# Seven-product multiplication in the up projection of a first MLP, with plain pairs in front that make its factors

## The reference

```python
h2 = rms_norm(x, ffn_norm)
u = causal_dwconv(h2 @ w_up, conv_w, conv_b)      # w_up: 1024 x 5632, three taps along the tokens
a, bval = jnp.split(u, 2, axis=-1)
return x + (jax.nn.silu(a) * bval) @ w_down       # w_down: 2816 x 1024
```

## Time and profile before

| | |
|---|---|
| Time, median of 3 runs (lowest to highest) | 1718.55 us (1718.5 to 1719.16) |
| The profiled execution: own time, span | 1718.6 us, 1716.8 us |
| TensorE matmul busy | 1704.7 us (99%), 9425 matmuls |
| TensorE weight loads | 1440.6 us (84%) |
| VectorE, ScalarE, GpSimd busy | 62%, 51%, 56% |
| Granted TensorE clock, mean | 0.999 |
| Mean transfer rate | 98 GB/s |

### The profile page before, as it was taken

How to read it: one execution, slowest core, us unless ns; L and a number is a source line. 1 busy time by engine, 2 the same in 40 slices (tenths; PEclk the granted TensorE clock), 3 DMA queues, 4 the chain that set the end, 5 groups by cost and what they waited for, 6 DMA issues and landing times.

```text
span 1716.8 us, 27243 instructions
## 1 busy us (share of the span) xinstructions
PE 1704.7 (99%) x9425; PEld 1440.6 (84%) x9425; DVE 1061.0 (62%) x2084; ACT 868.3 (51%) x1498; POOL 963.1 (56%) x1095
## 2 busy tenths in 40 slices
PE   9999999999999999999999999999999999999998
PEld 7778888888888778888989898977777889898988
DVE  6875755555311455568757575867776676757576
ACT  5665555555322444435545444546655554545355
POOL 5543655555555434357666666755554665656666
PEclk9999999999999999999999999999999999999999
DMA  5221333332334322223323323233322242333332
GB/s 192 74 68 61 100 98 98 97 93 93 108 95 137 104 68 83 74 74 123 99 98 99 105 96 106 64 128 116 105 97 70 87 133 91 109 99 98 99 98 74
DMA packets 48662, 167.91 MB, mean 98 GB/s; under 512 B 5376, under 2 KB 6672, under 8 KB 48528
## 3 DMA queue, kind: packets, MB, share of 16 engines
q1 hardware_dynamic: 48272, 166.05, 30.2%
q10 hardware_dynamic: 288, 0.52, 0.1%
HBM read 164.31 MB, written 2.24 MB: 97 GB/s over the span
## 4 chain that ended last, share of the span: by engine, by line
PE 90%; DVE 6%; ACT 2%; issue 1%; DMA 0%; POOL 0%; SPq 0%; DVEq 0%; ACTq 0%
PE bank L736 18%; PE bank L1444 6%; PE bank L1453 6%; PE bank L1445 6%; PE bank L661 5%; PE bank L660 5%; PE bank L666 5%; PE bank L1033 5%; PE bank L1034 5%; PE bank L1038 5%; PE bank L754 3%; PE bank L760 3%; PE bank L755 3%; PE bank L1086 2%; PE bank L1081 2%; PE bank L1080 2%
## 5 line engine op out<-in xcount | busy, mean ns | idle before, releaser
L507 POOL TENSOR_TENSOR w_lo<-stage,w_hi 128x256 fp32r<-128x256 f32 x872 | 672.2, 803 | 571.7 <-ACT w_hi L1506 317.5
L1506 ACT ACTIVATE w_hi<-stage 128x1024 fp32r<-128x1024 f32 x218 | 229.4, 1052 | 200.9 <-PE bank L1081 54.7
L660 PE MATMUL bank<-xn_hi,w_hi 128*128 128x512 f32 x544 | 211.8, 389 | 0.0
L661 PE MATMUL bank<-xn_lo,w_hi 128*128 128x512 f32 x544 | 211.7, 389 | 0.0
L736 PE MATMUL bank<-xn_hi,w_hi 128*128 128x512 f32 x464 | 189.1, 407 | 0.0
L736 PE MATMUL bank<-xn_lo,w_hi 128*128 128x512 f32 x464 | 181.8, 392 | 0.0
L2890 DVE TENSOR_TENSOR x<-x,bank 128x256 f32<-128x256 f32 (+1 forms) x217 | 97.4, 455 | 89.3 <-PE bank L1453 86.6
L1453 PE MATMUL bank<-arena 128*128 128x256 f32 x896 | 146.6, 283 | 0.0
L1033 PE MATMUL bank<-xn_hi,w_hi 128*128 128x512 f32 x352 | 137.1, 389 | 0.0
L1034 PE MATMUL bank<-xn_lo,w_hi 128*128 128x512 f32 x352 | 136.9, 389 | 0.0
L666 PE MATMUL bank<-xn_hi,w_lo 128*128 128x512 f32 x544 | 135.0, 389 | 0.0
(11 more groups left out here) (374 smaller groups left out, 3719.3 us busy)
## 6 DMA issues: line engine op xcount, KB each, us to landing
stage<-weights SPq DMA_DIRECT2D x219, 512.0 KB, 3.6
prob<-pairs SPq DMA_DIRECT2D x32, 512.0 KB, 3.6
stage<-pairs SPq DMA_DIRECT2D x32, 512.0 KB, 3.6
bias<-table SPq DMA_DIRECT2D x11, 896.0 KB, 6.4
out<-y SPq DMA_DIRECT2D x8, 256.0 KB, 2.2
x<-x_in SPq DMA_DIRECT2D x3, 512.0 KB, 7.6
bias<-swa_table SPq DMA_DIRECT2D x4, 256.0 KB, 4.4
con<-consts SPq DMA_DIRECT2D x1, 640.0 KB, 9.8
```

The lines of the kernel that those rows point to most:

```text
L507: ins = nc.gpsimd.tensor_tensor(w_lo[:, p_, ks], stage[:, p_, ks], w_hi[:, p_, ks].bitcast(F32), ALU.subtract)
L660: pe.matmul(G[p_][:], w_hi[:, p_, k], hi[:, k], start=(first and k == ks[0]), stop=False)
L661: mm = pe.matmul(G[p_][:], w_hi[:, p_, k], lo[:, k], start=False, stop=False)
L1506: act.activation(w_hi[:, p_], stage[:, p_], ACT.Copy).then_inc(hi_ready, 1)
```

## The change

Five of the 22 up pairs stay as they were. The other 17 become "quads": a pair's weights, 1024 by 256, are taken as four blocks of 512 by 128, the activations as four blocks of 512 features by 256 tokens, and seven products of 4 x 3 matmuls of 256 columns take the place of 48 matmuls of 512.

- During plain pairs 0 to 3 the activations' factors are made, one block of features a pair: VectorE multiplies two blocks of `x` by the norm's weight and rstd (already scaled, so the quads need no scaling) and forms four differences (`factors_first`, `factors_second`); ScalarE copies them to high parts (`factor_highs`, 256 and 1536 columns); VectorE (256 and 512 columns) and GpSimd (1024 columns in one instruction) make the low parts in the next pair.
- In a quad VectorE forms four sums of weight blocks and two low parts, ScalarE seven high parts and a copy, GpSimd five low parts. TensorE makes the products in the order `UP_ORDER` in four regions of PSUM. ScalarE copies four of them out, VectorE adds four (`c_00`, `c_01`, `c_1`), and the convolution follows.
- GpSimd multiplies the halves (`f_made_of`) instead of VectorE. Results stay in float32 and are split only at the end (`f_high`, `f_low`), since the factors lie where the parts will go. The first down tile therefore runs its matmuls of high and low weights by high results first and all those by low results last.
- The `Fori` loops of this stage are written out.

The core of the diff (indentation reduced):

```diff
-N_UP1 = 2 * NF1
+N_PLAIN = 5
+FACTORS_AT = [0, 1, 2, 3]
+Q_UP = NF1 - N_PLAIN
+N_UP1 = 2 * N_PLAIN
...
+UP_ORDER = [HI_A11, HI_S1, HI_A12, HI_S2, HI_S4, HI_A22, HI_S3]
+SLOT_ORDER = [HI_A11, HI_S1, HI_A12, HI_S2, HI_S4, HI_S3, HI_A22]
...
+factor = arena[:, N_IN_ARENA:2 * NF1].rearrange("p (c a r) s -> p c a (r s)", c=7, a=2)
+factor_parts = [arena_raw[:, 6:10].rearrange("p k s -> p (k s)"), v_tok[:].rearrange("p a b t f -> p (a b t f)")]
...
+f_home = [arena[:, N_IN_ARENA + 4 * c + b] for c in F_FREE for b in range(4)]
+f1_hi = f_home[0:NF1]
...
+def factor_lows(k):
+
+    pool.wait_ge(ffh_ready, 2 * k + 2)
+    ks = slice(k * HS, (k + 1) * HS)
+    nc.gpsimd.tensor_tensor(factor[:, F_T1:, 1, ks], factor_parts[k % 2][:, 2 * S:].rearrange("p (c s) -> p c s", c=4),
+                            factor[:, F_T1:, 0, ks].bitcast(F32), ALU.subtract).then_inc(factor_low, 1)
...
+def f_made_of(i):
+
+    pool.wait_ge(silu_done, i + 1)
+    pool.wait_ge(conv_2, 2 * i + 2)
+    nc.gpsimd.tensor_tensor(f1[i], conv_acc(i, 0), conv_acc(i, 1), ALU.mult).then_inc(f_made, 1)
...
+for i in range(N_PLAIN - 1):
+    split_lo(T_MLP1 // 2 + i + 1, 0)
+    if i:
+        f_made_of(i - 1)
+    if i - 1 in FACTORS_AT:
+        factor_lows(FACTORS_AT.index(i - 1))
+    split_lo(T_MLP1 // 2 + i + 1, 1)
+f_made_of(N_PLAIN - 2)
+if N_PLAIN - 2 in FACTORS_AT:
+    factor_lows(FACTORS_AT.index(N_PLAIN - 2))
...
+for q in range(Q_UP):
+    up_low(HI_S3, q)
+    if q == 0:
+        up_low(HI_A22, 0)
+    if q + 1 < Q_UP:
+        up_low(HI_A11, q + 1)
+    else:
+        split_lo(T_DOWN1 // 2, 0)
+        split_lo(T_DOWN1 // 2, 1)
+    f_made_of(N_PLAIN + q - 1)
+    if q + 1 < Q_UP:
+        for k in (HI_A12, HI_S4, HI_A22):
+            up_low(k, q + 1)
...
+def up_product(q, k):
+
+    region = R2 if k in (HI_A12, HI_A22) else R5 if k in (HI_S1, HI_S4) else R1[q % 2][:, 0:HS]
+    fresh = k in (HI_A11, HI_S1, HI_A12, HI_A22)
...
+    pe.wait_ge(slot_high, UP_HIGH_AT[k, q])
+    if k == HI_A11:
+        if q == 0:
+            pe.wait_ge(ffh_ready, FFH_PREP)
+            pe.wait_ge(ff_ready, FF_PREP)
+            pe.wait_ge(tab_sb, 2)
+        if q < 2:
+            pe.wait_ge(conv_2, 2 * (N_PLAIN - 2) + q + 1)
+        else:
+            pe.wait_ge(up_moved, moved_at(q - 2, U3_COPY))
+    elif k == HI_S1:
+        if q == 0:
+            pe.wait_ge(factor_low, QUADS)
+        else:
+            pe.wait_ge(product_added, 4 * (q - 1) + C_01)
+    elif k == HI_A12 and q:
+        pe.wait_ge(product_added, 4 * (q - 1) + C_10)
+    elif k == HI_S2:
+        pe.wait_ge(up_moved, moved_at(q, P1_COPY))
+    elif k == HI_S4:
+        pe.wait_ge(up_moved, moved_at(q, P5_COPY))
+    elif k == HI_A22:
+        pe.wait_ge(product_added, 4 * q + C_00)
+    elif k == HI_S3:
+        pe.wait_ge(up_moved, moved_at(q, U2_COPY))
+    for i in range(QUADS):
+        w, cols = up_hi[k][:, i * P:(i + 1) * P], slice(i * HS, (i + 1) * HS)
+        pe.matmul(region, w, factor[:, f, 0, cols], start=(fresh and i == 0), stop=False, skip_group_check=True)
+        pe.matmul(region, w, factor[:, f, 1, cols], start=False, stop=False, skip_group_check=True)
+    if k in UP_SUM_LOW:
+        pe.wait_ge(sum_made, N_SUM * q + UP_SUM_LOW[k])
+    else:
+        pe.wait_ge(slot_low, UP_LOW_AT[k, q])
+    for i in range(QUADS):
+        w, cols = up_lo[k][:, i * P:(i + 1) * P], slice(i * HS, (i + 1) * HS)
+        mm = pe.matmul(region, w, factor[:, f, 0, cols], start=False, stop=(i == QUADS - 1), skip_group_check=True)
+    mm.then_inc(product_done, 1)
...
+for i in range(1, N_PLAIN):
+    for p_ in range(2):
+        up_tile(i, p_)
+for q in range(Q_UP):
+    for k in UP_ORDER:
+        up_product(q, k)
...
+    if d == 0:
+        for s_, ks in pieces:
+            for k, f in ks:
+                if f in POOL_LOWS:
+                    pe.wait_ge(factor_low, QUADS + POOL_LOWS.index(f) + 1)
+                else:
+                    pe.wait_ge(ff_ready, FF_PREP + DVE_LOWS.index(f) + 1)
+                mm = pe.matmul(G[0][:], down_hi(T_DOWN1 + s_)[:, k], f1_lo[f], start=False, stop=(f == NF1 - 1))
+            mm.then_inc(hi_free if ks[-1][0] == KD - 1 else down_done, 1)
...
+def factor_highs(k):
+
+    act.wait_ge(factor_made, k + 1)
+    ks = slice(k * HS, (k + 1) * HS)
+    act.activation(factor[:, F_B11, 0, ks], factor_parts[k % 2][:, 0:HS], ACT.Copy).then_inc(ffh_ready, 1)
+    act.activation(factor[:, F_B21:, 0, ks], factor_parts[k % 2][:, S:].rearrange("p (c s) -> p c s", c=6),
+                   ACT.Copy).then_inc(ffh_ready, 1)
...
+def p5_copied(q):
+    act.wait_ge(product_done, N_PROD * q + UP_AT[HI_S1])
+    act.wait_ge(conv_2, 2 * (N_PLAIN + q))
+    if q == Q_UP - 1:
+        act.wait_ge(sum_made, N_SUM * q + UP_SUM_LOW[HI_S1])
+    act.activation(up_bank(N_PLAIN + q, 1)[:, HS:S], R5, ACT.Copy).then_inc(up_moved, 1)
...
+split_hi(T_MLP1 // 2 + 1, 0)
+for i in range(N_PLAIN - 1):
+    conv_0_of(i, 0)
+    silu(i)
+    split_hi(T_MLP1 // 2 + i + 1, 1)
+    conv_0_of(i, 1)
+    if i < N_PLAIN - 2:
+        split_hi(T_MLP1 // 2 + i + 2, 0)
+    if i in FACTORS_AT:
+        factor_highs(FACTORS_AT.index(i))
+act.wait_ge(tables_saved, 80)
+up_copy(0)
+act.wait_ge(ff_ready, FF_PREP)
+act.wait_ge(factor_low, QUADS)
+up_high(HI_A11, 0)
+conv_0_of(N_PLAIN - 1, 0)
+for k in (HI_S1, HI_A12, HI_S2, HI_S4):
+    up_high(k, 0)
+up_copy(1)
+for q in range(Q_UP):
+    i, more = N_PLAIN + q, q + 1 < Q_UP
+    if q:
+        u3_copied(q - 1)
+    if not more:
+        split_hi(T_DOWN1 // 2, 1)
+    silu(i - 1)
+    if q == 0:
+        conv_0_of(i - 1, 1)
+    up_high(HI_S3, q)
+    p1_copied(q)
+    if q:
+        conv_0_of(i - 1, 1)
+    else:
+        up_high(HI_A22, 0)
+    if more:
+        up_high(HI_A11, q + 1)
+    else:
+        f_high(0)
+        f_high(1)
+    p5_copied(q)
+    if more:
+        up_high(HI_S1, q + 1)
+        up_high(HI_A12, q + 1)
+    else:
+        for f in range(2, 6):
+            f_high(f)
+    u2_copied(q)
+    if more:
+        up_high(HI_S2, q + 1)
+        up_high(HI_S4, q + 1)
+    else:
+        f_high(6)
+        f_high(7)
+        f_high(8)
+    conv_0_of(i, 0)
+    if more:
+        up_high(HI_A22, q + 1)
+    if q + 2 < Q_UP:
+        up_copy(q + 2)
...
+def factors_first(k):
+
+    e = factor_parts[k % 2]
+    if k >= 2:
+        dve.wait_ge(ffh_ready, 2 * (k - 1))
+        dve.wait_ge(ff_ready, 2 * (k - 1))
+        dve.wait_ge(factor_low, k - 1)
+    b11, b12, b21, b22, t1, t3, t2, t4 = parts(k)
+    dve.scalar_tensor_tensor(out=e[:, 0:S], in0=x[:, k], scalar=pcol("ffn_norm", k, k + 1), in1=rstd[:],
+                             op0=ALU.mult, op1=ALU.mult)
+    dlink(dve.scalar_tensor_tensor(out=e[:, S:2 * S], in0=x[:, k + 4], scalar=pcol("ffn_norm", k + 4, k + 5), in1=rstd[:],
+                                   op0=ALU.mult, op1=ALU.mult))
+    dve.tensor_tensor(t1, b12, b11, ALU.subtract)
+    dlink(dve.tensor_tensor(t3, b22, b12, ALU.subtract))
+
+def factors_second(k):
+
+    b11, b12, b21, b22, t1, t3, t2, t4 = parts(k)
+    dlink(dve.tensor_tensor(t2, b22, t1, ALU.subtract))
+    dve.tensor_tensor(t4, b21, t2, ALU.subtract).then_inc(factor_made, 1)
...
+def c_00(q):
+
+    dve.wait_ge(up_moved, moved_at(q, P1_COPY))
+    dve.wait_ge(product_done, N_PROD * q + UP_AT[HI_A12])
+    dve.wait_ge(conv_2, 2 * (N_PLAIN + q) - 1)
+    if q == Q_UP - 1:
+        dve.wait_ge(sum_made, N_SUM * Q_UP)
+    dve.tensor_tensor(up_bank(N_PLAIN + q, 0)[:, 0:HS], p1_copy, R2, ALU.add).then_inc(product_added, 1)
...
+for i in range(N_PLAIN - 1):
+    scaled(i, 0)
+    conv(i, 0)
+    if i - 1 in FACTORS_AT:
+        factor_lows(FACTORS_AT.index(i - 1))
+    if i in FACTORS_AT:
+        factors_first(FACTORS_AT.index(i))
+    scaled(i, 1)
+    conv(i, 1)
+    if i in FACTORS_AT:
+        factors_second(FACTORS_AT.index(i))
+scaled(N_PLAIN - 1, 0)
+if N_PLAIN - 2 in FACTORS_AT:
+    factor_lows(FACTORS_AT.index(N_PLAIN - 2))
+for k in (HI_S1, HI_S3, HI_S2, HI_S4):
+    up_sum(0, k)
+conv(N_PLAIN - 1, 0)
+up_sum_low(0, HI_S1)
+up_sum_low(0, HI_S2)
+for q in range(Q_UP):
+    i, more = N_PLAIN + q, q + 1 < Q_UP
+    if q:
+        c_1(q - 1)
+    else:
+        scaled(i - 1, 1)
+        conv(i - 1, 1)
+    if more:
+        up_sum(q + 1, HI_S1)
+        up_sum(q + 1, HI_S3)
+        up_sum(q + 1, HI_S2)
+    if q:
+        conv(i - 1, 1)
+    c_00(q)
+    if more:
+        up_sum(q + 1, HI_S4)
+        up_sum_low(q + 1, HI_S1)
+        up_sum_low(q + 1, HI_S2)
+    else:
+        for f in range(3):
+            f_low(f)
+    c_01(q)
+    if not more:
+        f_low(3)
+    conv(i, 0)
+f_low(4)
+c_1(Q_UP - 1)
+f_low(5)
+f_low(6)
+conv(NF1 - 1, 1)
+for f in DVE_LOWS[7:]:
+    f_low(f)
+dve.wait_ge(f_made, NF1)
```

406 lines of the change are left out of this document (296 added, 110 removed).

## The result

The changed kernel takes 1727.76 us (median of 5 runs, 1726.84 to 1728.53), the kernel before 1718.58 us beside it (1718.5 to 1719.16): a ratio of 1.0052, 95% interval 1.004 to 1.0063. It is slower by half a per cent, inside the range of 1710 to 1729 and on the side that had the largest chance, but 5 us above the forecast of 1722.7. The profiled execution took 1727.2 us, with a span of 1725.4 (before: 1716.8). So 8.6 us have to be found.

What follows compares the result with a forecast made beforehand. TensorE was taken to bound the kernel (90% of the chain of waits). Against 1718.6 us, -13.8 + 12.0 + 3.4 + 1.4 + 1.0 = +4.0 us, forecast 1722.7 us, range 1710 to 1729.

Steps and rivals of the forecast that it cites:

- TensorE's saving: Up stage: 17 pairs at 10.89 us become seven products at 10.08 us, saving 13.8 us if TensorE never waits.
- The plain pairs: Factor-making pairs: a VectorE-ScalarE loop of 14.1 us delays the first product from 253.5 to 265.5, costing 12.0 us.
- rival C: Plain pairs: VectorE stands for GpSimd's whole instruction once in each of three loops, 6.9 us more, 1729.6 us; chance 0.09.
- Rival A: Plain pairs: small disturbance, first product only 3 to 6 us late, total faster at 1712.8 us; chance 0.33.
- The first two quads: Start of the quads: TensorE waits 2.4 us, then about 1.3, for VectorE's additions and copy; 3.4 us, ends 1 and 5.
- The steady quads: Remaining 15 quads: an engine-order loop of 10.17 us against TensorE's 10.08, costing 1.4 us, ends 0 and 6.
- The first down tile: First down tile: VectorE's low parts end at 12 to 17 us, TensorE wants the last at 15; 1.0 us, ends 0 and 3.
- the sign of being wrong: First down tile: the forecast is wrong if it takes over 3 us more than 66 x 0.227.

Runs made afterwards that it cites:

- n7: Seven plain pairs instead of the changed kernel's five, factors still made in pairs 0 to 3; 1721.32 us.
- n7_last: Changed kernel with seven plain pairs, factors in 0, 1, 3, 4, later high parts, low parts on VectorE, down-tile reordering and early matmuls, earlier weight split; 1711.91 us.
- highs_later: Changed kernel with ScalarE making a factor block's high parts behind the next pair's first convolution term instead of ahead of it; 1729.64 us.
- awake: Changed kernel with thirty unused matmuls behind the last plain pair, keeping TensorE busy during its wait before the first product; 1727.82 us.
- pieces: Changed kernel with GpSimd's 1024-column low-part instruction for a factor block cut into four of 256 columns; 1727.93 us.
- end_order: Changed kernel with all results' low parts on VectorE, and VectorE's last quad addition and ScalarE's high part of result 11 moved earlier; 1726.36 us.
- n6: Six plain pairs instead of the changed kernel's five, factors still made in pairs 0 to 3; 1728.80 us.

## Why the prediction was right, and where it was not

**TensorE's saving** was right: one product starts each 1.44 us, and the steady quads have no gap.

**The plain pairs** were right in mechanism: a closed loop through VectorE and ScalarE, slowed by GpSimd, sets the first product. That the start came out so close (265.5 against 264.97) is partly luck, as three parts were off in both directions. The last differences of pair 0 were done at 215.2 and not at 218.2: the convolution ended 0.7 us earlier, nothing disturbed that pair, where 1.8 was put in, and its steps took 0.5 less. The three loops behind it took 44.3 us (16.2, 13.8 and 14.2, to 259.4) and not 42.3, as one of them paid rival C's price. The way from there to the first product took 5.5 and not 5.0. Inside a loop the two terms were off as well: the loop alone is 11.0 and not 11.7, the disturbance 2.8 and not 2.4. n7 and n7_last show that this delay was the cost ahead of the steady quads. Rival A ("the disturbance is small") is out; rival C's mechanism is real, and how often it strikes hangs on small shifts of timing: a small move of ScalarE's order (highs_later) made it happen three times.

**The first two quads**: 3.4 predicted, 3.1 measured. The first loses 2.1 us (277.19 - 264.97 - 10.08; predicted 2.4, less the 0.3), the second 1.0, nearly all at its fifth product (predicted 1.3). The wait in the first came one product earlier than foretold, for ScalarE's copy, which stands behind the silu and a convolution term. From the changed kernel's trace alone the lower clock looked like the cause of the first one's loss, since the first product takes 1.3 us too long; awake shows that it was not.

**The steady quads**: 1.4 predicted, none measured. The step that failed is the 0.89 us between two convolution steps. In the written-out code they start 0.77 to 0.79 us apart (341.88 and 342.65 in a steady quad); two such steps in the loop make it 0.2 us shorter, which closes the 10.17 inside 10.08. That the register instruction which stood between the two steps before made the difference is argued from the order of instructions, not tested. In the steady quad of these rows VectorE waits 0.28 us for a copy that itself waits for TensorE, so TensorE sets the pace there.

**The first down tile** is the term that was mis-sized: 1.0 predicted, ends 0 and 3, measured 7.8 with what follows. Three of its numbers failed. "At 0.6 to 1.0 us each" was 1.36 beside GpSimd: the prediction knew of the disturbance and had priced it in the plain pairs, but took here the undisturbed cost with a little on top, although GpSimd works through nearly all of the same stretch. "When the last convolution ends some 5 us into the tile" was 7.5, for the same reason, as three disturbed low parts (1.2 to 1.5 us each) stand ahead of it. And ScalarE's high parts did not "run about level": TensorE waited 1.15 us for result 11 and lost another 1.3 over the next five, at a granted clock of 1.00. What the prediction named as the sign of being wrong, over 3 us more than 66 x 0.227, is what happened.

**The range** held by 1.2 us. The down tile was 6.8 us over its term and 4.8 over its upper end of 3. That the total still lies inside is owed to the other terms, which came out 2.2 us under theirs (11.5 for 12.0, 3.1 for 3.4, 0 for 1.4), and to luck.

## What to carry to other kernels

Where VectorE and GpSimd both subtract operands that lie in SBUF, add their times instead of taking the longer one, and give the work to the engine that does it in less time, even if that one is the fuller: three more instructions on VectorE made the tile 1.8 us shorter. A preparation that is a chain through several engines has a length of its own; price it against the work ahead of its consumer, and cover it with more of the old work (0.8 us a pair here) or spread it, before shortening its links one by one. When a wait is taken away, ask in the trace what stood behind it: highs_later, pieces, awake and end_order each took one away or made it shorter, and gained nothing.

## What the hardware showed that was not expected

- The same wait has not the same price each time. A wait of 1.9 us before the matmul at 251 was followed by matmuls 0.43 us apart (clock 0.68 in the window from 252 to 256) in n7, and also in awake (0.58), but not in the changed kernel, where that window shows 1.00. In n7 and in n6 eight matmuls were slow, 1.6 us where nothing hides it.
- Medians of kernels with such waits need more runs: the eleven of n7 lie within 2.9 us, the five of n7_last, which has none ahead of the first product, within 0.6. It is no rule, as the five of end_order, which has them, lie within 0.3.
- Which of VectorE and GpSimd is 0.05 us ahead decides about 2.2 us for an instruction of 512 columns beside one of 1024. The rows of highs_later above show GpSimd ahead (VectorE 2.90 for 0.68). In the changed kernel's last factor block VectorE is ahead, and GpSimd pays, 0.46 us over its 2.40:

```profile
261.30 0.69 DVE L2849 TENSOR_TENSOR arena<-v_tok,arena 128x512 fp32r<-128x512 f32 x1 [0.92 <-ACT arena L2006]
261.34 2.86 POOL L707 TENSOR_TENSOR arena<-v_tok,arena 128x1024 fp32r<-128x1024 f32 x1 [2.18 <-ACT arena L2006]
```
